# Attention kernel: VectorE makes a compressed step's row sums in front of reading the next step's scores

## The chip, the cores and the metric

The kernel runs on one core of one Trainium2 chip. The metric is the time of one execution on the device, in microseconds (us); lower is better.

## The reference

The program is a two-layer network on 1024 tokens of width 1024, all in float32: a mixer of linear attention and state space, a convolutional feed-forward net, a sparse attention mixer, a second feed-forward net, a last norm. The change lies in the sparse attention mixer. There, 16 heads in two groups share keys and values by group, and each query attends three times:

- compressed: to 63 keys, each made of a block of 32 tokens. `p_c = softmax(s_c)`, `o_c = p_c v_cmp`. The sum of `p_c` over the 8 heads of a group also says which blocks the query selects.
- selected: to the 6 best blocks of 64 tokens.
- window: to the last 512 tokens.

The three outputs are weighted by gates and added.

## The kernel before

Queries are taken in tiles of 128. The attention is a list of 144 steps, and a hand-written order runs over it. A step is either a compressed one, code 2 (one query tile, all 8 heads of a group, scores of 128 x 504), or a pair of heads with one query tile, in the window (code 1) or in the selected blocks (code 0). The first 80 steps mix 16 compressed steps with 64 window steps; the other 64 are selected ones. Compressed steps stand at places 4, 5, 9, 13, 17, 21, 25, 29, 33, 37, 41, 45, 49, 53, 57 and 61 of the list; the text calls them the first to the sixteenth. So the step behind a compressed one is a window step, but for the first, which has the second behind it.

What one step p goes through, and on which engine:

- TensorE makes the scores into PSUM (`scores`, lines 3101 and 3113). Each head of the next step overwrites the same PSUM banks, so scores of step p+1 wait for VectorE's reads of step p (`neg_ready`).
- VectorE reads them (`bias_step`). For a window step that is two instructions of line 2281, one for each head: add the bias, keep the row's extreme. For a compressed step it is `cmp_front`: add (2195), maximum (2198), clamp (2200), subtract (2201); GpSimd multiplies by the slopes (942).
- ScalarE takes exponentials: line 1513 for a compressed step, line 1519 for a head of a window step.
- VectorE then makes reciprocals of the sums (`norm_step`). A window step has its sums from ScalarE and needs one small instruction (2292). A compressed step needs `cmp_back`: sum over the keys (2207), clamp (2208), reciprocal (2209). It waits for the exponential (`p_ready`).
- GpSimd scales: line 965 for each head of a window step; for a compressed step `scale_step` has two instructions, 953 (times reciprocal) and 956 (times gate).
- TensorE turns the scaled scores by transposes, up to four tiles a group (`turn`, line 3134, which waits for `scaled`); ScalarE copies each group to SBUF (1532); TensorE multiplies by the values (3147 compressed, 3153 others). VectorE adds the product into the output (`out_step`).

`cmp_sum` (2215) is one more instruction of VectorE for each compressed step, the sum over heads.

Each engine executes its own list of instructions in order. TensorE goes in batches of two groups: first the scores for which the middle of a step lies in the batch, then two turns, then two products of values. VectorE goes by slots. A slot lies at the middle group of step p (`middle`), with AHEAD = 3:

```python
if p + AHEAD < len(steps):
    bias_step(p + AHEAD)
if steps[min(p + AHEAD - 2, len(steps) - 1)][0] == 2:
    cmp_sum(p + AHEAD - 2)
if p + AHEAD - 1 < len(steps):
    norm_step(p + AHEAD - 1)
```

So in one slot VectorE first reads the scores of step p+3 and then makes the sums of step p+2. Behind that come pieces of the selection of blocks in some slots (`importance`, `select`, lines 2246 to 2260), and `out_step` of an older step. GpSimd goes by `slope_step(p + 3)`, then `scale_step(p + 2)`.

Of the kernel before, what the change touches and what calls it, by code (L numbers as in the profile page):

```python
# [6 lines left out]
def hybrid_nsa_program(nc, x, norm_mix, norm_ffn, norm_final, hy_w_in, gdn_conv, gdn_a_log, gdn_dt_bias,  # L7
# [38 lines left out]
    with ctx:  # L46
# [84 lines left out]
        waiting, steps = [], [(1, 2 * m, (7,0,6,1,5,2,4,3)[0]) for m in range(OPENING)]  # L131
# [30 lines left out]
        BATCH, LAG, AHEAD = 2, 2, 3  # L162
# [1402 lines left out]
        def _(dve):  # L1565
# [607 lines left out]
            def block_rules(part):  # L2173
                if part == 0:
                    dve.wait_ge(ndc_ready, 4)
                    link(dve.tensor_scalar(MUL, VI, -1.0, None, ALU.is_lt))
                elif part == 1:
                    link(dve.tensor_scalar(ADD, VI, -1.0, 1e9, ALU.is_ge, ALU.mult))
                elif part == 2:
                    link(dve.tensor_scalar(VI, VI, 0.0, -2e9, ALU.is_gt, ALU.mult))  # L2180
                elif part == 3:
                    link(dve.tensor_tensor(ADD, ADD, VI, ALU.add))
                else:
                    link(dve.memset(MUL[:, :, 0:1], 0.0))
                    link(dve.memset(ADD[:, :, 0:1], 1e9))
# [17 lines left out]
            def cmp_back(p):  # L2203

                rs = CST[:, cmp_no[p] % 2, 1, :]
                dve.wait_ge(p_ready, 2 * p + 2)
                link(dve.tensor_reduce(out=rs, in_=scores_of(p), op=ALU.add, axis=AX.X))
                link(dve.tensor_scalar(rs, rs, 1e-30, None, ALU.max))
                dve.reciprocal(rs, rs).then_inc(r_ready, 1)

            def cmp_sum(p):

                b, h, qt = steps[p]
                dve.wait_ge(scaled, 2 * p + 1)
                dve.tensor_reduce(out=IMPP[:, (h // JH) * TT + qt, 1:1 + NC], in_=CPN.rearrange("p h n -> p n h"), op=ALU.add,
                                  axis=AX.X).then_inc(imp_c, 1)
# [19 lines left out]
            def importance(g, part):  # L2236
                v = IMP[:, g * TT:(g + 1) * TT, :]
                if part == 0:
                    dve.wait_ge(imp_c, (g + 1) * TT)
                    link(dve.tensor_tensor(v, cols(g, 1), cols(g, 2), ALU.add))  # L2240
                    link(dve.tensor_tensor(v, v, cols(g, 3), ALU.add))
                elif part == 1:
                    link(dve.scalar_tensor_tensor(out=v, in0=v, scalar=2.0, in1=cols(g, 0), op0=ALU.mult, op1=ALU.add))
                    link(dve.tensor_tensor(v, v, cols(g, 4), ALU.add))
                else:
                    link(dve.tensor_tensor(v, v, MUL, ALU.mult))
                    link(dve.tensor_tensor(v, v, ADD, ALU.add))

            def select(k, part):

                v = IMP[:, 2 * k:2 * k + 2, :]
                if part == 0:
                    vi, vj = v.unsqueeze(3).broadcast_to([P, 2, NB, NB]), v.unsqueeze(2).broadcast_to([P, 2, NB, NB])
                    link(dve.tensor_tensor(RGT, vj, vi, ALU.is_gt))
                    link(dve.tensor_tensor(REQ, vj, vi, ALU.is_equal))
                elif part == 1:
                    link(dve.tensor_tensor(REQ, REQ, TRI.unsqueeze(1).broadcast_to([P, 2, NB, NB]), ALU.mult))
                    link(dve.tensor_tensor(RGT, RGT, REQ, ALU.add))
                else:
                    link(dve.tensor_reduce(out=v, in_=RGT, op=ALU.add, axis=AX.X))  # L2260
                    dve.tensor_scalar(BB[:, 2 * k:2 * k + 2, :], v, 5.5, -BIG, ALU.is_ge, ALU.mult).then_inc(bb_ready, 1)

            def bias_step(p):

                b, h, qt = steps[p]
                if b == 2:
                    cmp_front(p)
                    return
                w = keys_of(qt, b)[1] * P
                if b == 0:  # L2270
                    dve.wait_ge(selb_ready, 2 * ((p - SELECTED) // PER_COUPLE) + 2)
                    bias = selected_bias(p)
                else:
                    dve.wait_ge(wb_ready, 1)
                    bias = NDW[:, 640 - w:640]
                if scores_free[p]:
                    dve.wait_ge(tr_done, pair_groups[scores_free[p]])
                for i in range(2):
                    n = 2 * p + i
                    dve.wait_ge(sc_ready, n + 1)  # L2280
                    dve.tensor_tensor_reduce(out=score_buf(p, i, 0, w), in0=score_ps(p, n % 2)[:, 0:w], in1=bias, scale=-slopes[h + n % 2],  # L2281
                                             scalar=3e38, op0=ALU.add, op1=ALU.min,
                                             accum_out=STAT[:, 0, n % 8:n % 8 + 1]).then_inc(neg_ready, 1)

            def norm_step(p):
                b, h, qt = steps[p]
                if b == 2:
                    cmp_back(p)
                    return
                at = (2 * p) % 8  # L2290
                dve.wait_ge(p_ready, 2 * p + 2)
                dve.reciprocal(STAT[:, 2, at:at + 2], STAT[:, 1, at:at + 2]).then_inc(r_ready, 1)  # L2292

            def out_step(p):
                b, h, qt = steps[p]
                if b == 2:
                    cmp_out(p)
                    return
                dve.wait_ge(pv_done, pair_groups[p + 1])
                if p >= 1:  # L2300
                    dve.wait_ge(o_used, p)
                o, src = OACC[:, h // 2, chunk(qt)], PS[:, 6 + p % 2, 0:P]
                if p < OPENING:
                    dve.tensor_copy(o, src).then_inc(o_used, 1)
                else:
                    dve.tensor_tensor(o, o, src, ALU.add).then_inc(o_used, 1)

            def out_lower_part(p):

                b, h, qt = steps[p]  # L2310
                dve.wait_ge(ot_hi, p - SELECTED + 1)
                dve.tensor_tensor(YL[:, h // 2, chunk(qt)], OACC[:, h // 2, chunk(qt)], OHI[h // 2][:, chunk(qt)].bitcast(f32),
                                  ALU.subtract).then_inc(y_ready2, 1)

            def ends(g):
                return g >= 0 and (g + 1) in pair_groups
# [9 lines left out]
            for k in range(pair_groups[-1]):  # L2326
                if k in middle:
                    p = middle[k]
                    if p + AHEAD < len(steps):
                        bias_step(p + AHEAD)  # L2330
                    if steps[min(p + AHEAD - 2, len(steps) - 1)][0] == 2:
                        cmp_sum(p + AHEAD - 2)
                    if p + AHEAD - 1 < len(steps):
                        norm_step(p + AHEAD - 1)
                    for g in range(NG):
                        if p in rank_at[g]:
                            importance(g, rank_at[g].index(p))
                    if p in select_at:
                        select(*select_at[p])
                    if p % 4 == 1 and 1 <= p // 4 <= 5:  # L2340
                        block_rules(p // 4 - 1)
                if ends(k - LAG):
                    out_step(group_step[k - LAG])
                    if group_step[k - LAG] - 4 >= SELECTED:
                        out_lower_part(group_step[k - LAG] - 4)
# [918 lines left out]
```

## Time and profile before

| | |
|---|---|
| three timed runs | 2923.2, 2934.16, 2935.76 us, median 2934.16 |
| the profiled execution | 2929.95 us, its span 2928.2 us |
| busy share of the span | TensorE 96%, VectorE 50%, ScalarE 38%, GpSimd 55% |
| stretch of the 16 compressed steps | about 1600 to 1850 us of the span |
| stretch of the selected steps | about 1890 to 2140 us of the span |

The profile is of one execution, and times in it count from the start of its span. "Idle before" of an instruction is time in which its engine stood still just before it, and the name behind the arrow is what ended it. The ends of matrix products are modelled. PEclk is the clock that TensorE was granted, as a share of 2.4 GHz.

### The profile page before, as it was taken

What the parts mean: (1) busy time and instruction counts of PE and PEld (TensorE: products, weight loads), DVE (VectorE), ACT (ScalarE), POOL (GpSimd) and SP (SyncE); (2) the same over time, 40 slices, a digit from 0 to 9 for tenths busy, and PEclk for the clock granted to TensorE, in tenths of its full rate; (3) what the DMA queues carried; (4) which work ended last, traced back from release to release, by engine and by line L of the source; (5) the groups of instructions that cost most, each with busy time, mean ns of one, the idle gap of its engine ahead of it and who ended that gap; (6) DMA issues with size and microseconds to landing.
All of it is one profiled execution on the core that took longest, in us unless ns stands there. A gap on an engine that the chain in (4) does not pass through costs nothing.

```text
span 2928.2 us, 43684 instructions
## 1 busy us (share of the span) xinstructions
PE 2823.5 (96%) x16887; PEld 2275.1 (78%) x16887; DVE 1451.8 (50%) x2276; ACT 1115.7 (38%) x1940; POOL 1607.9 (55%) x1194
## 2 busy tenths in 40 slices
PE   6998899999999999999999998999999999999998
PEld 5887877887888888888787666666677888888887
DVE  5555554442955555431401677755526745556325
ACT  3434442231444444100201565777723444443001
POOL 2454524554777776444533554545536777775442
PEclk9999999999999999999999998999999999999999
DMA  4110011122132223321421000000012222224311
GB/s 149 44 30 2 9 37 43 30 72 58 50 95 86 86 86 111 122 89 48 125 72 29 1 2 2 1 2 1 16 30 58 73 85 86 86 82 156 103 49 70
DMA packets 225246, 173.92 MB, mean 59 GB/s; under 512 B 10424, under 2 KB 209597, under 8 KB 224957
## 3 DMA queue, kind: packets, MB, share of 16 engines
q1 hardware_dynamic: 223469, 171.47, 19.1%
q8 instruction: 113, 1.85, 0.3%
q14 instruction: 48, 0.39, 0.0%
q10 hardware_dynamic: 1616, 0.21, 0.0%
HBM read 136.00 MB, written 31.46 MB: 57 GB/s over the span
## 4 chain that ended last, share of the span: by engine, by line
PE 87%; DVE 6%; POOL 3%; ACT 2%; issue 2%; DMA 0%; SPq 0%; DVEq 0%; POOLq 0%; ACTq 0%
PE PS L2383 28%; PE PS L2976 25%; PE PS L3113 5%; PE PS L3134 4%; PE PS L3153 4%; PE PS L2689 3%; PE PS L3187 3%; PE PS L3029 1%; PE PS L2531 1%; PE PS L2425 1%; DVE X L2281 1%; DVE X L1896 1%; DVE X L1684 1%; PE PS L2514 1%; PE PS L2411 1%
## 5 line engine op out<-in xcount | busy, mean ns | idle before, releaser
L636 POOL TENSOR_TENSOR WH<-WR,ONES 128x1024 fp32r<-128x1024 f32 (+1 forms) x108 | 251.7, 2331 | 636.2 <-PE PS L2383 441.8
L642 POOL TENSOR_TENSOR WL<-WR,WH 128x1024 fp32r<-128x1024 f32 (+1 forms) x116 | 286.8, 2472 | 19.1 <-ACT WH L1412 10.3
L2383 PE MATMUL PS<-YH,WH 128*128 128x512 f32 x864 | 269.9, 394 | 3.3 <-POOL WL L642 2.3
L965 POOL TENSOR_SCALAR X<-X,STAT,SM 128x640 f32<-128x640 f32 (+6 forms) x215 | 179.0, 841 | 168.8 <-DVE STAT L2292 168.7
L2383 PE MATMUL PS<-YL,WH 128*128 128x512 f32 x864 | 267.6, 391 | 0.0
L2383 PE MATMUL PS<-YH,WL 128*128 128x512 f32 x864 | 267.3, 391 | 0.0
L1532 ACT ACTIVATE Z<-PS 128x512 f32<-128x512 f32 (+2 forms) x336 | 176.6, 541 | 149.8 <-PE PS L3134 148.8
L2033 DVE SCALAR_TENSOR_TENSOR X<-PS,PTF,X 128x1023 f32<-128x1023 f32 (+1 forms) x176 | 221.4, 1278 | 14.5 <-ACT X L1357 4.3
L2383 PEld LDWEIGHTS PS<-YH,WH 128*128 128x128 f32 x864 | 161.7, 188 | 39.3 <-issue 3.6
L2383 PEld LDWEIGHTS PS<-YH,WL 128*128 128x128 f32 x864 | 163.2, 189 | 34.3
L2383 PEld LDWEIGHTS PS<-YL,WH 128*128 128x128 f32 x864 | 162.7, 188 | 34.3
L3113 PE MATMUL PS<-X 64*128 64x512 f32 (+3 forms) x768 | 172.9, 506 | 14.6 <-DVE STAT L2281 11.9
L835 POOL TENSOR_TENSOR WL<-WR,WH 128x512 fp32r<-128x512 f32 x108 | 139.9, 1296 | 76.0 <-ACT WH L1379 75.9
L2976 PE MATMUL PS<-YH,WH 128*128 128x512 f32 x456 | 177.4, 389 | 0.0
L2976 PE MATMUL PS<-YL,WH 128*128 128x512 f32 x456 | 177.4, 389 | 0.0
L2976 PE MATMUL PS<-YH,WL 128*128 128x512 f32 x456 | 177.4, 389 | 0.0
L3134 PE MATMUL PS<-IDENT,X 128*128 128x128 f32 (+1 forms) x988 | 153.9, 290 | 10.8 <-POOL X L956 5.9
L1519 ACT ACTIVATE X<-X,STAT 128x640 f32<-128x640 f32 (+6 forms) x215 | 157.6, 733 | 13.9 <-DVE STAT L2281 13.6
L3134 PEld LDWEIGHTS PS<-IDENT,X 128*128 128x128 f32 (+1 forms) x988 | 111.3, 144 | 61.6 <-issue 32.0
L3153 PE MATMUL PS<-Z,X 128*64 128x128 f32 x2112 | 153.8, 285 | 0.0
L835 POOL TENSOR_TENSOR WXL<-X,WXH 128x512 fp32r<-128x512 f32 x108 | 138.9, 1295 | 10.8 <-POOL X L850 5.1
L3113 PEld LDWEIGHTS PS<-X 64*128 64x128 f32 x768 | 82.8, 192 | 73.6 <-issue 42.2
(481 smaller groups left out, 6639.1 us busy)
## 6 DMA issues: line engine op xcount, KB each, us to landing
WR<-in_ffn_w_up_dram SPq DMA_DIRECT2D x88, 512.0 KB, 5.0
mid_scratch<-X SPq DMA_DIRECT2D x44, 512.0 KB, 2.6
WR<-in_hy_w_in_dram SPq DMA_DIRECT2D x28, 512.0 KB, 3.8
WR<-in_ffn_w_down_dram SPq DMA_DIRECT2D x32, 448.0 KB, 3.7
X<-mid_scratch SPq DMA_DIRECT2D x28, 512.0 KB, 4.7
Z<-mid_scratch SPq DMA_DIRECT2D x16, 512.0 KB, 7.7
WR<-in_ffn_w_down_dram SPq DMA_DIRECT2D x16, 512.0 KB, 3.8
WR<-in_nsa_w_in_dram SPq DMA_DIRECT2D x14, 512.0 KB, 3.8
```

The costliest lines, as they stand in the source:

```text
L636: pool.tensor_tensor(WH[:, slot, 0:k, :], raw[:, slot, 0:k, :], ONES[:, :].unsqueeze(1).broadcast_to([P, k, P]), ALU.mult).then_inc(w_hi, 1)
L642: pool.tensor_tensor(WL[:, slot, 0:k, :], raw[:, slot, 0:k, :], WH[:, slot, 0:k, :].bitcast(f32), ALU.subtract).then_inc(w_split, 1)
L835: pool.tensor_tensor(dst, whole, upper.bitcast(f32), ALU.subtract).then_inc(st_lo, 1)
L965: pool.tensor_scalar(score_buf(p, i, 0, w), score_buf(p, i, 0, w), STAT[:, 2, n % 8:n % 8 + 1], GATE[:, qt, gate:gate + 1], ALU.mult, ALU. ...
L1519: act.activation(score_buf(p, i, 0, w), score_buf(p, i, 0, w), ACT.Exp, scale=-1.0, bias=STAT[:, 0, n % 8:n % 8 + 1], accum_out=STAT[:, 1, ...
L1532: act.activation(PTR[g % len(PTR)][0:rows, 0:w], PS[0:rows, 4 + g % 2, 0:w], ACT.Copy).then_inc(pt_sb, 1)
L2033: dve.scalar_tensor_tensor(out=X[:, CG + s, d:], in0=ps[:, 0:SEQ - d], scalar=col(j + (C_FCONV + l * 6 * FT + (2 - d) * 2 * FT + s * FT)), ...
L2383: ins = pe.matmul(PS[:, bank + 2 * slot + a, :], w[:, slot, i, :], y[:, i, a * HALF:(a + 1) * HALF], start=(nth == 0 and w is WH and y is ...
L2976: ins = pe.matmul(PS[:, b + bank, :], w[:, i, :], y[:, i, :], start=first and not adds, stop=final, skip_group_check=True)
L3113: ins = pe.matmul(score_ps(p, i)[:, a:e], X[part, h // 2, chunk(qt)], X[part, kt, first * P + a:first * P + e], start=True, stop=True)
L3134: ins = pe.transpose(PS[0:rows, 4 + g % 2, (k - 4 * i) * P:(k - 4 * i + 1) * P], src, IDENT[:, :])
L3153: ins = pe.matmul(PS[head_part(k), 6 + p % 2, 0:P], X[:, (VS, VW)[b], (first + t) * P + (h // JH) * DH:(first + t) * P + (h // JH) * DH + DH],
```

## The change

Where the step whose sums are due in a slot (p+2) is a compressed one, `norm_step` comes first in the slot, in front of `bias_step(p + 3)` and of `cmp_sum`. In all other slots the order stays. No instruction is added or removed, and no other engine's list changes.

```diff
                 if k in middle:
                     p = middle[k]
+                    back_first = p + AHEAD - 1 < len(steps) and steps[p + AHEAD - 1][0] == 2
+                    if back_first:
+                        norm_step(p + AHEAD - 1)
                     if p + AHEAD < len(steps):
                         bias_step(p + AHEAD)
                     if steps[min(p + AHEAD - 2, len(steps) - 1)][0] == 2:
                         cmp_sum(p + AHEAD - 2)
-                    if p + AHEAD - 1 < len(steps):
+                    if p + AHEAD - 1 < len(steps) and not back_first:
                         norm_step(p + AHEAD - 1)
```

## Rows read from the trace of the kernel before

**Rows 1.** The page's busy times, and the shares by engine of the chain that ended last.
```profile
PE 2823.5 (96%) x16887; PEld 2275.1 (78%) x16887; DVE 1451.8 (50%) x2276; ACT 1115.7 (38%) x1940; POOL 1607.9 (55%) x1194
...
PE 87%; DVE 6%; POOL 3%; ACT 2%; issue 2%; DMA 0%; SPq 0%; DVEq 0%; POOLq 0%; ACTq 0%
```

**Rows 2.** Busy time by stretch: length, busy us of each engine, PEclk, DMA.
```profile
1600.00:1850.00 250.00, 227.65 (x2080) 167.40 (x2080) 183.11 (x488) 148.80 (x364) 132.19 (x153) 0.92 0.01 1
```

**Rows 3.** TensorE's waits, 1600 to 1890 us: total us, times, longest us.
```profile
PE PS L3113 <- DVE STAT L2281: 6.6, 11, 1.1
PE PS L3134 <- POOL X L956: 5.9, 5, 2.1
...
PE PS L3134 <- POOL SRX L956: 3.0, 2, 1.6
```

**Rows 4.** Timeline, fifth compressed step: start, us, engine, line, what [idle before, releaser].
```profile
1659.04 0.62 ACT L1513 ACTIVATE X<-X 128x504 f32<-128x504 f32 x1 [0.91 <-POOL X L942]
...
1660.62 0.82 DVE L2281 CUSTOM_DVE_ANT_0 SRX<-PS,X 128x640 f32<-128x640 f32 x1 [2.13 <-PE PS L3113]
...
1662.12 0.67 DVE L2207 TENSOR_REDUCE CST<-X 128x8 f32<-128x504 f32 x1
...
1663.31 1.03 POOL L953 TENSOR_TENSOR Z<-X,CST 128x504 f32<-128x504 f32 x1 [3.29 <-DVE CST L2209]
...
1663.53 0.66 PE L3134 MATMUL PS<-IDENT,X 128*128 128x128 f32 x4
...
1664.42 1.03 POOL L956 TENSOR_TENSOR X<-Z,SM 128x504 f32<-128x504 f32 x1
...
1665.60 0.29 PE L3134 MATMUL PS<-IDENT,X 128*63 128x128 f32 x1 [1.41 <-POOL X L956]
```

**Rows 5.** Timeline, sixth compressed step.
```profile
1674.31 0.83 DVE L2281 CUSTOM_DVE_ANT_0 X<-PS,X 128x640 f32<-128x640 f32 x1 [0.23 <-PE PS L3113]
...
1674.62 0.62 ACT L1513 ACTIVATE X<-X 128x504 f32<-128x504 f32 x1 [1.76 <-POOL X L942]
...
1675.80 0.67 DVE L2207 TENSOR_REDUCE CST<-X 128x8 f32<-128x504 f32 x1
...
1675.90 1.38 PE L3113 MATMUL PS<-X 64*128 64x512 f32 x8
1676.43 0.23 PEld L3113 LDWEIGHTS PS<-X 64*128 64x128 f32 x2 [0.20 <-issue]
...
1678.11 1.03 POOL L956 TENSOR_TENSOR X<-Z,SM 128x504 f32<-128x504 f32 x1
...
1679.67 0.54 PE L3134 MATMUL PS<-IDENT,X 128*63 128x128 f32 x3
```

**Rows 6.** Timeline behind the twelfth compressed step, VectorE and TensorE.
```profile
1763.75 1.40 DVE L2255 TENSOR_TENSOR Z<-Z 128x512 f32<-128x512 f32 x1
...
1766.28 0.48 PE L3113 MATMUL PS<-X 64*128 64x128 f32 x2 [1.14 <-DVE STAT L2281]
```

**Rows 7.** Timeline of TensorE, turns of the eleventh, thirteenth and fifteenth compressed step.
```profile
1750.85 0.62 PE L3134 MATMUL PS<-IDENT,X 128*63 128x128 f32 x4 [1.83 <-POOL X L956]
...
1787.00 0.62 PE L3134 MATMUL PS<-IDENT,SRX 128*63 128x128 f32 x4 [1.63 <-POOL SRX L956]
...
1818.58 0.76 PE L3134 MATMUL PS<-IDENT,X 128*63 128x128 f32 x4 [2.07 <-POOL X L956]
```

**Rows 8.** Timeline at the first two compressed steps: GpSimd and TensorE.
```profile
1616.56 1.03 POOL L942 TENSOR_TENSOR X<-X,SLOPE 128x504 f32<-128x504 f32 x1
...
1618.84 0.44 PE L3134 MATMUL PS<-IDENT,SRX 128*128 128x128 f32 x2 [1.04 <-ACT Z L1532]
```

**Rows 9.** Busy time by stretch, where PEclk fell.
```profile
1767.70:1781.40 13.70, 13.32 (x82) 10.25 (x82) 6.27 (x17) 5.40 (x13) 6.14 (x7) 0.50 0.00 0
...
1788.20:1791.60 3.40, 3.40 (x21) 2.23 (x16) 2.76 (x10) 2.09 (x7) 2.98 (x3) 0.50 0.02 5
...
1818.90:1822.30 3.40, 3.40 (x21) 2.12 (x20) 1.97 (x6) 1.96 (x5) 1.73 (x2) 0.50 0.00 0
```

## Prediction

> **What bounds the kernel now.** I read the page first. TensorE is busy 96% of the span and holds 87% of the chain that ended last [rows 1], so a change on VectorE counts only where TensorE stands still for it. The change touches 16 slots, all between 1600 and 1850 us. The table of stretches says that TensorE works 227.65 of these 250 us [rows 2]: 22 us of standing is all there is to win here, 0.8% of the whole. The list of waits says for whom it stands. Two of its rows, 5.9 and 3.0 us, are waits of a turn for GpSimd's line 956, the last work on a compressed step's scores; another, 6.6 us, is a wait of scores for VectorE's reads, line 2281 [rows 3]. The change moves a compressed step's sums in front of such reads. It can shorten the first two rows, and it lengthens the third. I then went through the timeline of all 16 compressed steps for one question: at the slot where sums and reads meet, which of their inputs comes first, the exponential (for the sums) or TensorE's scores (for the reads)? There are two patterns, and they alternate.
>
> **Pattern A, exponential first.** The fifth step stands for it [rows 4]. The exponential ends at 1659.04 + 0.62 = 1659.66. VectorE stands idle 2.13 us until the next step's scores come at 1660.62, reads them, and starts the sums only at 1662.12. GpSimd's 953 starts at 1663.31, after 3.29 us idle, and its 956 ends at 1665.45. TensorE has finished its turn before at 1664.19 and stands 1.41 us. Six steps are like this: the fifth, seventh, ninth, tenth, thirteenth and fifteenth.
>
> **Pattern B, scores first.** The sixth step stands for it [rows 5]. VectorE reads from 1674.31, and the exponential ends only at 1674.62 + 0.62 = 1675.24. The sums start at 1675.80, right behind the reads. 956 ends at 1679.14, and TensorE comes to that turn at 1679.67: it doesn't wait. The fourth, sixth, eighth, twelfth, fourteenth and sixteenth step are like this; the third and eleventh are near it. The reason for the alternation is that TensorE takes groups in batches of two: the scores behind a compressed step's come one batch later in B, two in A.
>
> **The change part by part.** No instruction is added or removed, no DMA is moved, and no queue of another engine changes. What is moved is three instructions of VectorE, 16 times. From the start of the sums to the start of 953 it is 1663.31 - 1662.12 = 1.19 us [rows 4]; without the handover between engines, taken at 0.08 (953 ends at 1664.34, 956 starts at 1664.42), the sums occupy VectorE 1.1 us.
>
> *A slots.* The sums start at 1659.66 + 0.08 = 1659.74 instead of 1662.12. 953 and 956 come 2.4 us earlier, 956 ends at 1663.1, before TensorE gets there at 1664.19: the stall of 1.41 goes. The reads start at about 1660.85, 0.2 us late. Queued behind them on VectorE are the rest of the slot, and on TensorE the scores that overwrite those banks; these come at 1661.99 in any case, after the first read's end at 1661.7, so the 0.2 costs nothing. What is late next is ScalarE's copy of the turned group, which comes behind two exponentials in its list; I therefore count 1.2 and not 1.41. The seventh step has the same 1.41. The thirteenth and fifteenth have 1.63 and 2.07 [rows 7], counted as 1.5 and 1.9. The ninth and tenth have no stall, so nothing to win. The eleventh, a near-B, stalls 1.83 [rows 7]; its sums can come 1.0 earlier, and I count 1.3, between 1.0 and the whole 1.83. Sum of gains: 1.2 + 1.2 + 1.5 + 1.9 + 1.3 = 7.1 us.
>
> *B slots.* Here the sums wait for the exponential, and the reads, whose scores lie ready, stand behind them. Sums from 1675.24 + 0.08 = 1675.32 to 1676.43; reads from there, not from 1674.31: 2.1 us late. The scores that wait for these reads started at 1675.90 for the first head and at 1676.43 for the second [rows 5]. The first read would end 0.83 later, at 1677.26, the second 0.75 after it, at 1678.0. TensorE's first head is then 1.4 us late, the second 1.6. Turns and values of that batch stand behind the scores in TensorE's list, so 1.6 us go into the path. Against it, 956 ends 0.5 earlier, where nobody waited. Four slots (fourth, sixth, eighth, sixteenth) at 1.6: 6.4 us. In the twelfth and fourteenth VectorE is itself late afterwards: it has a piece of the selection to do (1.40 us), and TensorE stands 1.14 us for the reads behind that [rows 6]. VectorE's own loss is only its idle wait, 2.1 - 1.1 = 1.0, and TensorE's stall of before takes up the rest: 1.0 each, 2.0 together.
>
> *The others.* In the third, ninth and tenth the two inputs come within 1 us of each other. A delay lies between 0 and B's 1.6; I take 1.1 for the three together, since they are nearer A. At the first two, the step whose reads are put behind is itself compressed. Its `cmp_front` comes later; GpSimd's list has the second step's 942 in front of the first's 953, and ScalarE has the second's exponential in front of copies for which TensorE already stands 1.04 us [rows 8]. 942 started at 1616.56; with the sums of the first from 1614.2 to 1615.3 and `cmp_front` behind them, it would start near 1617.6. That is 1.0 late, and it goes through to TensorE: 1.1, with ends at 0 and 2.1.
>
> Sum of losses: 6.4 + 2.0 + 1.1 + 1.1 = 10.6 us. Net: 10.6 - 7.1 = +3.5 us.
>
> One rule bears on all this. The trace shows VectorE in the order of its list where that was idle waste: 2.13 us idle with an input for the sums ready [rows 4]. By the Trainium skill, "PSUM — Partial Sum Buffer", section "Engine vs sequencer instructions", ScalarE's, VectorE's and GpSimd's queues are strictly first in, first out. By that rule, with which the row agrees, the wait put in front in B must hold the reads, and it speaks against the change; were it not so, both sums would be 0 and the time 2930.
>
> *The clock.* Stalls have a second price. TensorE's granted clock fell to 0.50, that is 1.2 GHz, behind three stalls: 13.7 us long behind that of the twelfth step's stretch, 3.4 us each behind those of the thirteenth and fifteenth [rows 6, 7, 9]; not behind the 1.41 of the fifth or the 1.83 of the eleventh. At half clock a bound TensorE loses half of the stretch: 6.8, 1.7 and 1.7. The change takes away the last two stalls, and 3.4 us of loss with them. It makes four new stalls of 1.6. Of the six turns or scores discussed that stood over 1.1 us (fifth, seventh, eleventh, twelfth, thirteenth, fifteenth), three had a fall, with a mean loss of 3.4; four new ones at that rate would cost 6.8, and at the rate of the two 1.41 stalls, which are the nearest, 0. I take 5. Net of the clock: +1.5, with ends at -3.4 and +24 (four long falls, 27.2 - 3.4).
>
> **Total:** 3.5 + 1.5 = +5 us on the profiled execution's 2929.95: 2935 us. That execution lies 4 us under the median of the three timed runs, 2934.16, and within their spread of 12.6 us. I leave the number at 2935, and call 0.5% (15 us) about what a measurement of this kernel can tell from no change.
>
> **The rivals.**
>
> *The reads' delay is hidden* (chance 0.13). TensorE may have other work or other waits that take up B's 1.6, and only the gains count, with the two falls of the clock gone: -7.1 - 3.4 = 2919.5 us. For it: some stalls for line 2281 exist anyway [rows 3] and could swallow a part. Against it: in B, TensorE took the scores at 1675.90 with no wait, and the next instruction of its list is behind them.
>
> *Nothing in sum* (0.17). The change doesn't do what it says where it counts: gains and losses are of one size, and the small terms may well cancel: 2930 us, within 2 us.
>
> *The new stalls bring the clock down* (0.08). Mechanism: TensorE stands 1.6 us in each B slot, and long falls like the one at 1767.7 follow. Each costs 6.8 us. From two long falls on, with the +3.5 and no fall saved, it is 3.5 + 13.6 = +17 us, 2947, over 0.5% slower; all four would be 2961. For it: a stall of 1.14 had such a fall [rows 6, 9]. Against it: the two stalls of 1.41 had none.
>
> My forecast, slightly slower and not measurable, has 0.62.
>
> **How the numbers follow.** The forecast's own range is 2929 to 2941. Around it lie the timed runs' spread, some 6 us either way, the first rival at 2919.5, and the third from 2947 on. 2922 to 2947 leaves out most of the third rival and a part of the first, together some 2 in 10. Faster by over 0.5% needs every gain, no loss, and luck: 0.03. Slower by over 0.5% is the third rival: 0.07. Within 0.5%: 0.90.
>
> **What would show it.** In A slots, line 2207 starts within 0.1 us of the end of 1513, and TensorE's waits for 956, 8.9 us together, shrink to under 2. In B slots, VectorE stands idle in front of 2207 for the exponential, and line 2281 starts about 2 us later; TensorE's waits for 2281 grow from 6.6 to some 15. In the stretch 1600 to 1850, TensorE's standing stays near 22 us, plus 3 or 4. The prediction is wrong if the waits for 2281 don't grow, if 956 still holds TensorE, or if PEclk in that stretch moves far from 0.92.

## The result, and the profile after

| | kernel before | changed kernel |
|---|---|---|
| median of 7 runs, us | 2931.18 | 2947.52 |
| lowest and highest, us | 2923.2 and 2935.76 | 2941.51 and 2952.34 |
| the profiled execution: time and span, us | 2929.95 and 2928.2 | 2946.41 and 2944.7 |

The ratio is 1.006, 95% interval [1.0046, 1.0074]: the change makes the kernel 16 us slower. The forecast was 2935, between 2922 and 2947, which was 5 us above its base of 2930, with 0.90 on no measurable difference. It was too low by some 12 us, and of the three outcomes the one that came had 0.07.

The page of the changed kernel, busy times. TensorE has as many instructions as before [rows 1] and is busy 15 us longer.

```profile
PE 2838.5 (96%) x16887; PEld 2282.5 (78%) x16887; DVE 1451.5 (49%) x2276; ACT 1115.3 (38%) x1940; POOL 1606.9 (55%) x1194
```

Nearly all of it arises in the stretch with the 16 slots: the attention begins 2.1 us later, and the selected steps begin 17.8 us later, at 1904.8 us for 1887.0. So the stretch that took 250 us [rows 2] takes some 16 more. The table of stretches for it, and three of its pieces at half clock (same columns as there):

```profile
1600.00:1867.00 267.00, 242.40 (x2088) 173.62 (x2088) 181.98 (x485) 148.30 (x364) 131.72 (x156) 0.89 0.01 1
...
1769.90:1780.10 10.20, 10.20 (x62) 7.18 (x61) 4.92 (x11) 2.42 (x6) 4.06 (x7) 0.50 0.00 1
1804.00:1814.20 10.20, 10.20 (x62) 7.45 (x60) 6.71 (x16) 2.70 (x7) 5.11 (x6) 0.50 0.00 1
1838.20:1848.40 10.20, 10.20 (x58) 7.51 (x60) 6.13 (x14) 2.95 (x7) 4.54 (x6) 0.50 0.01 2
```

The clock explains a part and not the whole. The kernel before had two more pieces at half clock beside the three of [rows 9]:

```profile
1600.45:1607.30 6.85, 6.21 (x21) 4.29 (x22) 2.75 (x8) 2.71 (x5) 1.27 (x2) 0.50 0.00 0
1627.80:1641.50 13.70, 13.48 (x72) 9.57 (x70) 8.32 (x27) 7.22 (x19) 7.42 (x9) 0.50 0.00 0
```

Its five pieces add up to 41 us. The changed kernel has eight in the same stretch: the three above, three of 6.8 and two of 3.4 us, 58 together. These 17 us more cost at most half of that, 8 to 9 us. Of the other 7 only a small part is standing: outside of TensorE's busy time there are 250 - 227.65 = 22.4 us before and 267 - 242.40 = 24.6 after, 2.2 more. The rest, some 5 us, counts as busy time; the B slot below shows where such time comes from, products that no longer run side by side.

TensorE's waits from 1600 to 1900 us (total us, times, longest) show that the waits for line 956 are gone, 8.9 us of them [rows 3], and what has come:

```profile
PE PS L3116 <- DVE STAT L2281: 9.6, 13, 1.8
PE PS L3137 <- ACT Z L1532: 3.9, 5, 2.2
...
PE PS L3137 <- POOL X L965: 3.8, 6, 0.9
PE PS L3137 <- POOL SRX L965: 3.8, 5, 1.1
```

(Lines below the changed place have moved by three: 3116 is 3113 of before, 3137 is 3134, 3156 is 3153.) Line 965, GpSimd's scaling of a window step, was hardly in that list before: 1.4 us in all. It has 7.6 now, 6.2 more, for the 8.9 that went. The waits for 2281, which the forecast had at some 15, rise from 6.6 to 9.6 only; a part of the reads' lateness lies inside of TensorE's busy time (the B slot below).

**An A slot after the change**: timeline at the fifth compressed step, to be read against [rows 4].

```profile
1667.79 0.62 ACT L1513 ACTIVATE X<-X 128x504 f32<-128x504 f32 x1 [0.91 <-POOL X L942]
...
1668.44 0.68 DVE L2207 TENSOR_REDUCE CST<-X 128x8 f32<-128x504 f32 x1 [1.20 <-ACT X L1513]
...
1669.64 1.03 POOL L953 TENSOR_TENSOR Z<-X,CST 128x504 f32<-128x504 f32 x1 [0.87 <-DVE CST L2209]
...
1670.75 1.03 POOL L956 TENSOR_TENSOR X<-Z,SM 128x504 f32<-128x504 f32 x1
...
1672.41 1.09 PE L3137 MATMUL PS<-IDENT,X 128*128 128x128 f32 x8
...
1673.10 0.60 ACT L1532 ACTIVATE Z<-PS 128x512 f32<-128x512 f32 x1 [1.60 <-PE PS L3137]
...
1673.60 0.82 ACT L1519 ACTIVATE SRX<-SRX,STAT 128x640 f32<-128x640 f32 x1
...
1673.94 1.08 DVE L2215 TENSOR_REDUCE Z<-Z 128x63 f32<-128x504 f32 x1
...
1674.93 0.17 DVE L2292 RECIPROCAL STAT<-STAT 128x2 f32<-128x2 f32 x1
...
1675.20 2.63 POOL L965 TENSOR_SCALAR SRX<-SRX,STAT,SM 128x640 f32<-128x640 f32 x3 [3.42 <-DVE STAT L2292]
...
1676.22 0.30 PE L3137 MATMUL PS<-IDENT,SRX 128*128 128x128 f32 x1 [0.70 <-POOL SRX L965]
...
1676.99 0.55 PE L3137 MATMUL PS<-IDENT,SRX 128*128 128x128 f32 x3 [0.47 <-POOL SRX L965]
```

The sums start as soon as 1513 ends, and 956 ends long before TensorE's turn at 1672.41, which goes on into this step's scores with no wait: that stall is gone as forecast. But the next turn, of the window step behind, stands twice for 965, 0.70 and 0.47 us. GpSimd itself waited 3.42 us for that step's reciprocal, 2292; 2292 stood behind the sum over heads, 2215, and needed an exponential of 1673.60 that ScalarE takes behind a copy (1532). In the kernel before that chain was as late, but TensorE came 1.4 us later and didn't see it: from the start of 1513 to the start of 965 it was 7.26 us there (the row below and [rows 4]), and it is 7.41 now.

```profile
1666.30 1.73 POOL L965 TENSOR_SCALAR SRX<-SRX,STAT,SM 128x640 f32<-128x640 f32 x2 [0.85 <-DVE STAT L2292]
```

**A B slot after the change**: timeline at the eighth compressed step, like the sixth in [rows 5].

```profile
1715.25 0.62 ACT L1513 ACTIVATE X<-X 128x504 f32<-128x504 f32 x1 [1.76 <-POOL X L942]
...
1715.90 0.68 DVE L2207 TENSOR_REDUCE CST<-X 128x8 f32<-128x504 f32 x1 [1.20 <-ACT X L1513]
...
1716.97 0.82 DVE L2281 CUSTOM_DVE_ANT_0 SRX<-PS,X 128x640 f32<-128x640 f32 x1
...
1717.72 0.82 DVE L2281 CUSTOM_DVE_ANT_0 SRX<-PS,X 128x640 f32<-128x640 f32 x1
...
1717.86 2.09 PE L3116 MATMUL PS<-X 64*128 64x512 f32 x8 [1.26 <-DVE STAT L2281]
...
1718.60 0.72 PEld L3116 LDWEIGHTS PS<-X 64*128 64x128 f32 x5 [0.45 <-DVE STAT L2281]
```

VectorE stands idle 1.20 us for the exponential with the next scores ready; then sums, then reads. TensorE stands 1.26 us for the first read; the weight loads of the second head (`PEld`) wait 0.45 us more for the second read, while products of the first head run. The eight products that took 1.38 us [rows 5] take 2.09, 0.71 more. The turn in front of them starts 12.60 us later than in the kernel before (1714.69 for 1702.09), the turn behind them 14.64 later (1719.87 for 1705.23): 2.04 us are lost here.

### The profile page after: what moved, and what is told of

Its sections match the earlier page's. It is cut to its first block, busy times and chain, and to the rows that moved or that the text cites. A ratio compares the mean times of both kernels' runs of the same rounds, so it can differ in the third digit from the quotient of the medians.

```text
span 2944.7 us, 43684 instructions
## 1 busy us (share of the span) xinstructions
PE 2838.5 (96%) x16887; PEld 2282.5 (78%) x16887; DVE 1451.5 (49%) x2276; ACT 1115.3 (38%) x1940; POOL 1606.9 (55%) x1194
## 4 chain that ended last, share of the span: by engine, by line
PE 86%; DVE 6%; POOL 3%; ACT 2%; issue 2%; DMA 0%; SPq 0%; DVEq 0%; ACTq 0%; POOLq 0%
PE PS L2386 28%; PE PS L2979 24%; PE PS L3116 5%; PE PS L3137 4%; PE PS L3156 3%; PE PS L2692 3%; PE PS L3190 3%; PE PS L3032 1%; PE PS L2534 1%; PE PS L2428 1%; DVE X L1896 1%; POOL X L965 1%; DVE X L2281 1%; DVE X L1684 1%; PE PS L2517 1%
## 5 line engine op out<-in xcount | busy, mean ns | idle before, releaser
L3116 PE MATMUL PS<-X 64*128 64x512 f32 (+3 forms) x768 | 179.7, 513 | 17.7 <-DVE STAT L2281 14.9
```

The costliest lines, as they stand in the source:

```text
L3116: ins = pe.matmul(score_ps(p, i)[:, a:e], X[part, h // 2, chunk(qt)], X[part, kt, first * P + a:first * P + e], start=True, stop=True)
```

## The experiments

Ten kernels, five rounds each, each with the kernel before on the same chip. None leaves out any of the computation; only orders differ. The ratios are as recorded with the runs, and not exactly those of the medians.

| run | median, us | before beside it | ratio [95% interval] |
|---|---|---|---|
| A slots alone | 2937.30 | 2932.11 | 1.0019 [1.0005, 1.0032] |
| B slots alone | 2938.72 | 2932.11 | 1.0023 [1.0012, 1.0035] |
| the four others alone | 2935.71 | 2932.11 | 1.0019 [1.0007, 1.0031] |
| the first two alone | 2935.52 | 2932.24 | 1.0010 [0.9997, 1.0022] |
| B slots, sums between the reads | 2930.65 | 2932.24 | 0.9994 [0.9981, 1.0007] |
| reciprocal behind A steps, no early sums | 2931.59 | 2932.24 | 0.9999 [0.9985, 1.0013] |
| A slots and that reciprocal | 2929.66 | 2932.11 | 0.9986 [0.9974, 0.9997] |
| the same, and ScalarE's order | 2925.60 | 2932.24 | 0.9980 [0.9967, 0.9992] |
| the same, and the eleventh step | 2925.40 | 2931.57 | 0.9981 [0.9972, 0.9991] |
| whole change, reciprocal, ScalarE's order | 2935.87 | 2931.57 | 1.0017 [1.0007, 1.0027] |

**The change in three parts.** One line chooses the steps for which the sums go in front:

```diff
-                    back_first = p + AHEAD - 1 < len(steps) and steps[p + AHEAD - 1][0] == 2
+                    back_first = p + AHEAD - 1 in (17, 25, 33, 37, 49, 57)      # A slots
+                    back_first = p + AHEAD - 1 in (13, 21, 29, 45, 53, 61)      # or: B slots
+                    back_first = p + AHEAD - 1 in (4, 5, 9, 41)                 # or: the others
```

> The sums go in front only at the six A slots (fifth, seventh, ninth, tenth, thirteenth, fifteenth compressed step); all other slots as before. Theory 1 (the win of 1.4 to 2.1 us at each of the four stalls is given back within one step, because the next turn then waits for GpSimd's line 965 of the window step behind): within 2 us of the kernel before; waits of TensorE for line 956 fall by some 6.5 us and waits for 965 grow by about as much. Recorded sum (the gains hold): 5.8 us faster, up to 9 if two falls of the clock go too.

> The sums go in front only at the six B slots (fourth, sixth, eighth, twelfth, fourteenth, sixteenth). Theory 1 (each B slot costs TensorE the whole lateness of the reads, 2.0 us): 10 to 12 us slower from the stalls alone, more with falls of the clock. Recorded sum: 8.4 us slower. Rival (the clock alone makes the loss): slower only in as far as stretches at PEclk 0.50 between 1600 and 1870 us are longer than the 41 us of before; with as much of them as before, within 3 us.

> The sums go in front only at the first two, the third and the eleventh compressed step. Theory 1: 3 to 6 us slower, nearly all of it at the first two, where the second step's front now stands behind the first's sums; the eleventh wins nothing. Recorded sum: within 1 us of the kernel before (1.1 lost at the first two, 0.6 at the third, 1.3 won at the eleventh).

The three losses add up: 0.19 + 0.23 + 0.19 = 0.61%, the whole change has 0.60. Each has an interval of some 0.13% either way, so the sum leaves room for some 8 us by which the slots act on each other. The four others, where the recorded sum had less than 1 us, lose 3.6 us by the medians; the first two of them follow below. And the A slots, on which the whole win rested, don't win. TensorE's waits in the run with the A slots alone:

```profile
PE PS L3137 <- POOL X L965: 4.1, 7, 0.9
...
PE PS L3137 <- POOL X L956: 3.6, 3, 1.7
PE PS L3137 <- POOL SRX L965: 3.2, 5, 1.1
```

956 falls from 8.9 to 3.6, 965 rises from 1.4 to 7.3: 5.3 us won, 5.9 lost. Of the 3.6 left, 1.64 stand at the third step, whose order is as before and where it was 0.22; so at the A slots themselves 6.7 us of standing went. In its trace the fifth step's turn comes 1.58 us earlier relative to the step before it, the two parts of the turn behind it 0.83 and 0.71 later, and the account stands at 0; the seventh has -1.58, +0.86, +0.71. That the run is then 5 us slower than before, and not equal, I had not expected; its mean granted clock over all runs is 0.9832 for 0.9844, which accounts for 3 to 4 us at most. The rest stays open.

The B slots cost, by the turns in their run's trace, 1.98, 2.05 and 2.05 us at the fourth, sixth and eighth step, where the forecast had 1.6 each; at the twelfth and fourteenth 2.04 and 1.98, of which 1.06 and 1.05 come back a turn later, so 1.0 each as forecast; at the sixteenth 1.3. Together 9.3 us for the 8.4 of the forecast. The whole run with them is 6.6 us slower, less than the 10 to 12 expected and with a clock no lower than before (0.985 for 0.984); in its trace PEclk from 1600 to 1870 us is 0.97, for 0.92 before. So the rival that the clock alone makes the loss falls for these slots: the run is slower with less time at half clock.

**The first two alone** (the line with `(4, 5)`).

> The sums go in front only at the first two compressed steps. Theory 1: nearly the whole loss of the run with the four remaining slots is here, 3 to 5 us slower. Recorded sum: 1.1 us slower, between 0 and 2.1.

3.3 us slower, with an interval that only just takes in no change. In its timeline the second step's `cmp_front` (2195) begins only at 1617.03, behind the first's sums; 942 follows at 1619.43, the second's exponential at 1620.55, and the turn that stood 1.04 us for ScalarE's copy [rows 8] stands 2.21:

```profile
1617.03 0.68 DVE L2195 TENSOR_TENSOR X<-PS,Z 128x504 f32<-128x504 f32 x1
...
1619.43 1.03 POOL L942 TENSOR_TENSOR X<-X,SLOPE 128x504 f32<-128x504 f32 x1 [1.14 <-DVE X L2201]
...
1620.55 0.62 ACT L1513 ACTIVATE X<-X 128x504 f32<-128x504 f32 x1 [3.36 <-POOL X L942]
...
1621.71 0.44 PE L3137 MATMUL PS<-IDENT,SRX 128*128 128x128 f32 x2 [2.21 <-ACT Z L1532]
```

**How much the lateness of the reads costs: half a dose.** At the B slots the sums go between the two heads' reads.

```diff
                     dve.tensor_tensor_reduce(... accum_out=STAT[:, 0, n % 8:n % 8 + 1]).then_inc(neg_ready, 1)
+                    if i == 0 and between is not None:
+                        norm_step(between)
...
-                        bias_step(p + AHEAD)
+                        bias_step(p + AHEAD, p + AHEAD - 1 if back_first else None)
```

> At the six B slots the sums go between the two reads instead of in front of both. Theory 1 (the cost is the lateness of the reads): the first read is not late, the second by 1.2 us, of which TensorE has about 0.4 to spare; each slot costs 0.8 instead of 2.0 us, together 5 us slower than before, against some 7 to 12 for the sums in front of both. Rival (the early sums themselves cost, through GpSimd's earlier start or the clock): as slow as the run with the B slots, 6 to 7 us.

In the trace, the sixth and eighth step's loss is 1.22 us each, between 0 (sums behind) and 2.05 (sums in front, in the run with the B slots alone): the cost goes with the lateness of the reads. Timeline at the sixth step:

```profile
1678.99 2.60 PE L3116 MATMUL PS<-X 64*128 64x512 f32 x8
...
1679.41 0.77 DVE L2281 CUSTOM_DVE_ANT_0 X<-PS,X 128x640 f32<-128x640 f32 x1
...
1680.24 0.30 PEld L3116 LDWEIGHTS PS<-X 64*128 64x128 f32 x4 [0.96 <-DVE STAT L2281]
```

The first head's product starts at once, the second's waits for a read that is late, and the eight products span 2.60 us, not 1.38. The time of the whole run doesn't show the 5 us that were expected: its median is 1.6 under that of the kernel before. But its mean clock is 0.9860 for 0.9833, which is some 16 us less at half clock and worth up to 8 us, enough to cover the 5. What the stalls cost by the trace and what the run shows are not the same thing here.

**Who takes over at the A slots.** If it is 965 of the window step behind, then an earlier 965 brings the win, and nothing without the early sums. The reciprocal (2292) goes in front of the sum over heads (2215) in the slot behind an A step:

```diff
+                    after_a = p + AHEAD - 2 in (17, 25, 33, 37, 49, 57)
+                    if after_a:
+                        norm_step(p + AHEAD - 1)
                     if steps[min(p + AHEAD - 2, len(steps) - 1)][0] == 2:
                         cmp_sum(p + AHEAD - 2)
...
```

> As the run with the A slots alone, and at the slot behind each of them the reciprocal of the window step that follows (line 2292) goes in front of the sum over heads (2215). If theory 1 is right that line 965 of that step takes over the stall, it starts about 0.5 us earlier at each of the A slots: 2 to 3 us less than the A slots alone, in sum 1 to 4 us faster than the kernel before. If the stall has another source, the same as the A slots alone, within 1 us.

> The sums stay behind the reads everywhere, as in the kernel before; only the reciprocal of the window step behind each of the six A steps (line 2292) goes in front of the sum over heads (2215). Theory 1 (line 956 ends last there, and line 965 only once 956 is early): no difference, within 2 us of the kernel before, with the 956 waits of 8.9 us still there; so the win of the run with both moves needs both. Rival (that win came from the reciprocal alone): some 3 us faster, as that run.

With the early sums at A: 0.14% faster, some 4 us (2.5 by the medians), an interval that only just leaves out no change; 965's waits are down from 7.3 to 3.1 us. Alone: no difference, with 9.0 us of waits for 956 still there. As theory 1 had it, the win needs both. The next link of the chain is ScalarE, which takes the second head's exponential between its copies:

```diff
+                after_a = ahead - 1 in (17, 25, 33, 37, 49, 57)
+                if after_a:
+                    exp_step(ahead, (1,))
                 evacuate(p, 0, (count + 1) // 2)
-                if ahead < len(steps):
+                if ahead < len(steps) and not after_a:
                     exp_step(ahead, (1,))
```

> As the run with the A slots and the reciprocal behind them, and ScalarE takes the exponential of the second head of that window step in front of its copies, not between them. Theory 1 (line 965 of the window step sets the turn behind an A step): 965 starts up to 0.8 us earlier again, and the waits for 965, 3.1 us in all, go: 2 to 3 us faster than that run, 5 us faster than before. Rival (ScalarE's copies are as late as 965, so the next wait is for line 1532): no faster than that run.

0.20% faster than before, 5.9 us. Timeline of this run behind the fifth step (here 2295 is the reciprocal, 3143 the turns):

```profile
1661.12 0.16 DVE L2295 RECIPROCAL STAT<-STAT 128x2 f32<-128x2 f32 x1
...
1661.38 1.74 POOL L965 TENSOR_SCALAR SRX<-SRX,STAT,SM 128x640 f32<-128x640 f32 x2 [2.43 <-DVE STAT L2295]
...
1662.04 0.65 PE L3143 MATMUL PS<-IDENT,X 128*63 128x128 f32 x4
...
1662.53 0.27 PE L3143 MATMUL PS<-IDENT,SRX 128*128 128x128 f32 x1
...
1663.17 0.55 PE L3143 MATMUL PS<-IDENT,SRX 128*128 128x128 f32 x3 [0.37 <-POOL SRX L965]
```

965 starts 0.7 us ahead of the compressed step's second turn (1661.38 for 1662.04); after the change alone it started 0.3 us behind the start of that turn (1675.20 for 1674.87). The row at 1662.53 is the first part of the window step's turn, which no longer waits; of the two stalls one of 0.37 us is left. Over 1600 to 1900 us the waits for 965 did not go, as expected, but fell from 3.1 to 2.4, and those for ScalarE's copies (1532) from 3.3 to 2.1. No run has ScalarE's order alone, and the intervals of this run and the one without it overlap, so what it adds by itself is not shown.

**Both together.** The two moves behind A steps are added to the whole change; and the eleventh step is treated like an A step in the best run.

> The whole change (all 16 slots), and behind the six A steps the two moves that make line 965 of the next window step earlier (reciprocal in front of the sum over heads, second exponential in front of ScalarE's copies). Theory 1: the A slots now keep their win also beside the slots that lose: 8 to 12 us faster than the whole change alone, 4 to 8 us slower than the kernel before. Rival (the two moves only help where no other slot is disturbed): within 3 us of the whole change, 14 to 17 us slower than before.

> As the run with the A slots and both moves behind them, with the eleventh step (near B, a stall of 1.83 us for line 956 before) treated like the A steps. Theory 1: the sums go in front about 1 us earlier there, the reads come up to 1.5 us late: a wash, within 2 us of that run, so 4 to 7 us faster than before. If the eleventh behaves like a clean A step: 2 us faster than that run.

The whole change with both moves is 0.17% slower than before where the whole change had 0.60: the two moves are worth some 12 us beside it, as theory 1 had it, and about as much as between the A slots alone (+0.19%) and the A slots with both moves (-0.20%). The eleventh step is a wash, as expected. The best kernel of the study is the one with early sums at A steps only and both moves, 0.2% faster than the kernel before.

## Why the prediction was wrong

Two terms failed: the gains at the A slots, 7.1 us that didn't come, and the price of the clock, 1.5 us for 8 to 9 at most. Point by point:

- *What bounds the kernel, and the two patterns*: right in the main. The slots behave as A and B, and every stall is TensorE's. Sums start within 0.1 us of the exponential's end in A, and VectorE idles for it in B. One reading was too large: of the 2.13 us that VectorE stood idle in A, the input for the sums was ready in the last 0.96 only (1659.66 to 1660.62 in [rows 4]); the order of the list shows in these as well.
- *A slots, the gains of 7.1 us*: the first step that failed, in its mechanism. "What is late next is ScalarE's copy of the turned group", it said, and took off 0.2 us for each. Late next was 965 of the window step behind, through 1532, 1519, 2215 and 2292, and it took the win back: 956's waits fell by 5.3 us in the run with the A slots alone (6.7 at these slots), 965's rose by 5.9, and at the fifth step the account stands at 0. The runs that make 965 earlier, with the early sums (0.14% and 0.20% faster) and without them (no difference), show that it is this chain.
- *B slots, 8.4 us*: the mechanism was right, and so was the 1.0 where VectorE itself was late afterwards; the 1.6 of the others measured 2.0 (1.3 in the last), 9.3 together. I had read the second head's scores as starting 0.53 us behind the first's [rows 5], and so as having that much to spare. They start together: the first four weight loads of the kernel before, of both heads, are at 1675.90 (below), just behind the second read, which ends at 1675.88. So the whole lateness counted, and the products of the two heads, which had run side by side, ran in part one behind the other.

```profile
1675.06 0.82 DVE L2281 CUSTOM_DVE_ANT_0 X<-PS,X 128x640 f32<-128x640 f32 x1
...
1675.90 0.33 PEld L3113 LDWEIGHTS PS<-X 64*128 64x128 f32 x4 [0.17 <-DVE STAT L2281]
```

- *The first two, 1.1 us*: the stall grew by 1.17 as worked out, and the run shows some 3 us (between -1 and +6.5), which doesn't rule out 1.1.
- *The eleventh, +1.3*: nothing measurable; in the best run it made no difference.
- *The clock, +1.5 net*: the second step that failed, in its size. It went by three falls of 20.5 us together, and left out the two at 1600.45 and 1627.80, as much again. The stalls that went were replaced by pairs of stalls for 965 one turn later, 1.63 us by 1.06 and 0.47 at the thirteenth step, 2.07 by 0.84 and 0.92 at the fifteenth. Falls of 10.2 us stand behind these pairs, at 1804.0 and 1838.2 us, where the kernel before had 3.4 each, and behind a like pair of the eleventh step, at 1769.9; the 13.7 us of before behind the twelfth [rows 9] are gone. In all 17 us more at half clock, 8 to 9 us at most. The rival "the new stalls bring the clock down" had the direction. Its size (+17 us) came out by luck, with 13.6 us of clock in it, and it had not the place: behind the four B slots it named, only the sixth step's had a fall at once, of 3.4 us, and the three longest falls each follow a pair of stalls for 965.
- *0.5% as what a measurement can tell*: too wide. With seven runs of each kernel the interval is 0.14% either way, so the 0.90 rested on a noise that isn't there.

In the two traces, of some 16 us, 2 are standing, at most 8 to 9 are clock, and the rest, some 5, are products that run longer. How it divides over the runs is open. Within the 35 runs of the kernel before that stand beside the first experiments, times go from 2921 us at a granted clock of 0.989 to 2939 at 0.982, so one and the same kernel moves with its clock by as much as the change moved it, and no run here holds the clock fixed.

## What to carry to other kernels

When a stall is to be taken away, follow the bound engine one more step: list what it needs in its next two instructions and when each of these is ready, and count as the win only the time to the next of them that is late. Putting work with an unmet input in front of work whose input lies ready cost the bound engine that whole lateness in the traces here; so such a reorder is for the slots where the trace shows the input ready, one by one, and not for all slots of a kind. Where a stall has a twin chain beside it, moving both is worth more than either: here neither early sums nor an early reciprocal won anything, and both won 0.14%, with ScalarE's order 0.20%.

## What the runs showed of the hardware

- Two heads' products on the two halves of the rows run side by side: eight took 1.38 us [rows 5], 2.09 when the second head's input came 0.74 us behind the first's, and 2.60 when it came 1.25 behind. A late second input costs the overlap too. By the Trainium skill, "TensorEngine Tiling (Array Packing)", section "Overview", the array can work as independent smaller tiles when the contracted dimension is at most 64; the trace agrees, with 1.38 us for the two heads together and 2.60 for one behind the other.
- Small stalls in a row can be followed by a granted clock of 1.2 GHz: behind 0.84 and 0.92 us for 965 at 1835 and 1836 us, it was 0.50 for 10.2 us (rows below, of the changed kernel). Behind the 1.41 us in one piece of [rows 4] it stayed at 1.00, and so it did behind the pair of 0.70 and 0.47 us at the changed kernel's fifth step. So the price of a stall is not told by its own length.

```profile
1835.26 0.30 PE L3137 MATMUL PS<-IDENT,X 128*128 128x128 f32 x1 [0.84 <-POOL X L965]
1836.47 0.55 PE L3137 MATMUL PS<-IDENT,X 128*128 128x128 f32 x3 [0.92 <-POOL X L965]
```

- A stall can hide behind the half clock. At the third step, whose order is the same in both, TensorE stands 0.22 us for 956 in the kernel before, at PEclk 0.50, and 1.64 us in the run with the A slots alone, at 1.00 (the two rows below, in this order). So what a fall costs and what stalls cost don't simply add up.

```profile
1635.64 1.08 PE L3134 MATMUL PS<-IDENT,X 128*63 128x128 f32 x4 [0.22 <-POOL X L956]
...
1636.26 0.62 PE L3137 MATMUL PS<-IDENT,X 128*63 128x128 f32 x4 [1.64 <-POOL X L956]
```

- One kernel's runs spread with the clock: the 35 runs of the kernel before that stand beside the first experiments lie in three groups, at 2921 to 2927, 2932 and 2936 to 2939 us; those beside the later ones cover the same range with less of a gap between. A single execution, such as the profiled one of the A slots alone (2926.29 us, median 2937.30), can lie 11 us from its median and on the other side of the comparison.
